# Routing from unnormed, weighted activations with the norm's factor applied per token, and a first gather in plain fp32

## What is computed

```python
for i in range(2):
    h = h + mixer_i(rmsnorm_2(h, norm_mix[i]))
    h = h + hier_moe(rmsnorm_2(h, norm_ffn[i]), ...)       # touched
    gate = sigmoid(rmsnorm_2(h, norm_ple[i]) @ w_ple_gate[i] + b_ple_gate[i])
    h = h + gate * (p[i] @ w_ple[i])

def rmsnorm_2(x, g):
    return x * rsqrt(mean(x * x, axis=-1) + EPS) * g

def hier_moe(x, w_rg, b_rg, w_re, b_re, w_gate, w_up, w_down):
    pg = softmax(x @ w_rg + b_rg)                # 4 groups, the best one is taken
    le = (x @ w_re + b_re) of that group         # 8 experts, the best two
    weight = pg_top * normalised(top_p)
    # each token's two experts: (silu(x @ w_gate[e]) * (x @ w_up[e])) @ w_down[e], weighted and summed
```

## Time and profile before

| | us |
|---|---|
| median of 3 runs | 1819.16 |
| lowest and highest | 1817.28, 1819.76 |
| the profiled execution, its own time | 1821.02 |
| its span in the trace | 1819.2 |
| PE busy | 1676.1 (92%) |
| DVE, ACT, POOL busy | 717.0, 512.0, 269.4 |
| mean granted TensorE clock | 0.965 |
| read from memory | 525.91 MB |

### The profile page before, as it was taken

One profiled execution on the slowest core, in us unless ns is written; L12 is line 12 of the kernel. 1 busy time (PEld: TensorE's weight loads), 2 busy tenths in 40 slices (PEclk: granted clock), 3 DMA queues, 4 the chain that ended last, 5 costly groups with the idle time before them and its releaser, 6 DMA issues.

```text
span 1819.2 us, 25704 instructions
## 1 busy us (share of the span) xinstructions
PE 1676.1 (92%) x10638; PEld 1141.4 (63%) x10638; DVE 717.0 (39%) x1356; ACT 512.0 (28%) x786; POOL 269.4 (15%) x165
## 2 busy tenths in 40 slices
PE   4989898999989999999999998897899999999986
PEld 2678597999989854454444545896655454443546
DVE  1466623899356531221212214667421221222224
ACT  3444334544343221111111114456211111111123
POOL 1405413477510010000000001000100000000010
PEclk9999979999999989999999999998999999999998
DMA  9203515343546759999999995333799999999960
GB/s 405 84 16 144 232 58 233 112 179 138 199 147 230 287 232 413 428 428 428 429 428 428 429 428 229 139 140 143 289 413 427 429 428 429 429 427 428 429 275 24
DMA packets 37516, 528.08 MB, mean 290 GB/s; under 512 B 4160, under 2 KB 4288, under 8 KB 4800
## 3 DMA queue, kind: packets, MB, share of 16 engines
q1 hardware_dynamic: 36864, 525.22, 69.9%
q10 hardware_dynamic: 576, 1.75, 0.2%
HBM read 525.91 MB, written 1.05 MB: 290 GB/s over the span
## 4 chain that ended last, share of the span: by engine, by line
PE 71%; DMA 16%; DVE 6%; ACT 5%; issue 1%; POOL 0%; SPq 0%; ACTq 0%; DVEq 0%
PE bank L500 24%; PE bank L988 18%; DMA ring<-in_w_up 13%; PE bank L1014 9%; PE bank L943 3%; PE bank L944 3%; PE bank L569 2%; PE bank L493 2%; PE bank L959 2%; DMA ring<-in_dense 2%; PE bank L960 1%; PE bank L1085 1%; DMA work<-in_dense 1%; PE bank L674 1%; ACT work L1443 1%
## 5 line engine op out<-in xcount | busy, mean ns | idle before, releaser
L988 PE MATMUL bank<-ring,work 128*64 128x512 f32 x1536 | 338.2, 595 | 14.6 <-DMA ring<-in_w_up 12.4
L500 PE MATMUL bank<-xn_rounded,ring_rounded 128*128 128x256 f32 (+1 forms) x2304 | 338.8, 290 | 9.4 <-DVE xn_rounded L1663 8.9
L500 PEld LDWEIGHTS bank<-xn_rounded,ring_rounded 128*128 128x128 f32 x2304 | 304.1, 196 | 14.7 <-issue 10.8
L988 PEld LDWEIGHTS bank<-ring,work 128*64 128x64 f32 x1536 | 112.6, 137 | 234.3 <-issue 220.6
L500 PE MATMUL bank<-work_rounded,ring_rounded 128*128 128x256 f32 (+1 forms) x1488 | 242.2, 297 | 12.4 <-DVE xn_rounded L1663 5.3
L1562 POOL TENSOR_TENSOR ring_rounded<-ring,ring_rounded 128x2048 fp32r<-128x2048 f32 (+1 forms) x43 | 187.0, 4369 | 292.9 <-ACT ring_rounded L1152 292.9
L500 PEld LDWEIGHTS bank<-work_rounded,ring_rounded 128*128 128x128 f32 x1488 | 208.1, 193 | 22.8 <-issue 7.9
L2140 DVE TENSOR_TENSOR work<-work,bank 128x512 f32<-128x512 f32 x32 | 22.0, 687 | 407.9 <-PE bank L988 407.9
L1014 PE MATMUL bank<-ring,work 128*64 128x512 f32 x768 | 170.1, 595 | 0.0
L1152 ACT ACTIVATE ring_rounded<-ring 128x2048 fp32r<-128x2048 f32 (+1 forms) x86 | 151.0, 1804 | 57.9 <-PE bank L500 36.0
L1632 POOL TENSOR_TENSOR work<-work_rounded,work 128x128 f32<-128x128 f32 x64 | 24.2, 399 | 838.4 <-PE bank L1007 831.4
(11 more groups left out here) (318 smaller groups left out, 1834.1 us busy)
## 6 DMA issues: line engine op xcount, KB each, us to landing
ring<-in_dense SPq DMA_DIRECT2D x50, 2048.0 KB, 8.6
ring<-in_w_gate SPq DMA_DIRECT2D x48, 2048.0 KB, 20.9
ring<-in_w_up SPq DMA_DIRECT2D x48, 2048.0 KB, 22.7
ring<-in_w_down SPq DMA_DIRECT2D x48, 2048.0 KB, 25.6
work<-in_w_gate SPq DMA_DIRECT2D x16, 2048.0 KB, 20.5
work<-in_w_up SPq DMA_DIRECT2D x16, 2048.0 KB, 24.1
work<-in_w_down SPq DMA_DIRECT2D x16, 2048.0 KB, 27.0
ring<-in_dense SPq DMA_DIRECT2D x8, 1408.0 KB, 6.2
```

Of the source, the lines that this page charges most:

```text
L500: last = mm(out, rv(ring[r][:, at:at + P]), rv(x[part][k]), start=k == 0 and j == 0, stop=k == n_k - 1 and j == 2)
L988: last = mm(b[64 * y:64 * y + 64, :], xg[:, k, 64 * y:64 * y + 64], ws[y][:, 512 * k:512 * k + 512], start=k == 0, stop=k == KT - 1)
```

## The change

- `add_output` (for `out_a` and `out_b`) now also makes the weighted, unnormed input hT * norm_ffn (two instructions behind each addition). `scaled` is no longer called ahead of the experts.
- The sums of squares become a column per 128 tokens: `token_sums` multiplies each 128 by 128 piece of squares with one column of ones. The reciprocal root is then 128 by 2 (`rstd_tok`).
- The first four tiles' sums and router products (`routing_ahead`) stand ahead of the last use of the projection.
- The logits are multiplied by `rstd_tok` per token where DVE adds the bias; the transposed tokens are multiplied by it in ACT's copy. That copy is fp32 alone. High and low parts are made behind the first gather (ACT and POOL), and wait for it.
- The first gather is 16 products in plain fp32. Two parts of the embedding stand ahead of it (one on each side of the rank products), two behind it.
- `select(0)` moves ahead of the overflow flag's five instructions and of six memsets; two casts, a copy and a subtraction go (a second table `iota1` in the constants, 32 KB more).
- `ple_w` gets a place of its own, and is loaded ahead of `odd`: in layer 0 once the first block's mixer has ended, in layer 1 once the first layer's experts have.
- Two semaphores of an earlier stage become one; its waits are the same.

```diff
-    ple_w, ple_sq, ple_xh = flat(2048, 2048), gsb, flat(0, 2048).rearrange("p (k t) -> p k t", k=KT)
+    ple_w, ple_sq, ple_xh = flat(17504, 2048), gsb, flat(0, 2048).rearrange("p (k t) -> p k t", k=KT)
...
-                sp.wait_ge(*((S["y_ready"], KT), (S["lru_var"], 3))[layer])
+                sp.wait_ge(*((S["h_ready"], KT), (S["moe_done"], 1))[layer])
                 sp.dma_start(ple_w, t["dense"][N_DENSE + layer][:, 0:2 * D]).then_inc(S["ple_w_load"], 16)
...
-            if layer:
-                load_embedding()
+            load_embedding()
             sp.wait_ge(*((S["h_ready"], 2 * KT), (S["lru_h"], KT))[layer])
             sp.dma_start(odd[0], gate[2]).then_inc(S["odd_full0"], 16)
             for c in order[len(early):]:
-                if layer == 0 and c == order[-2]:
-                    load_embedding()
                 load(base + c, (gate, up, down)[c // 2][c % 2], CHUNK)
...
-        projection("out_a", "w_out_a", 4, [[x[:, k] for k in range(KT)] for x in (yh, yT)], ("y_ready", 1), True)
+        w_r = par("w_router").rearrange("p (l k c) -> p l k c", l=2, k=KT)
+        def token_sums(tiles):
+            for k in tiles:
+                if k % 2 == 0:
+                    pe.wait_ge(S["sq_ready"], 4 * (count["norms"] + 1) + k // 2 + 1)
+                for u in range(NH):
+                    last = mm(bank[5][:, u:u + 1], sq1[:, k, P * u:P * u + P], ones[:, 0:1], start=k == u == 0,
+                              stop=k == KT - 1 and u == 1)
+            if tiles[-1] == KT - 1:
+                signal(last, "ss_ready")
+                count["norms"] += 1
+        def router(layer, tiles):
+            for k in tiles:
+                pe.wait_ge(S["xn_ready"], KT * n_normed[0] + k + 1)
+                last = mm(bank[7][0:36, 0:SEQ], w_r[:, layer, k], xs[k], start=k == 0, stop=k == KT - 1)
+            if tiles[-1] == KT - 1:
+                signal(last, "lg_mm")
+                n_normed[0] += 1
+        def routing_ahead(layer):
+            token_sums(early)
+            router(layer, early)
+        projection("out_a", "w_out_a", 4, [[x[:, k] for k in range(KT)] for x in (yh, yT)], ("y_ready", 1),
+                   lambda: routing_ahead(0))
...
-            ready = norm_input(late)
-            for b in range(BANKS):
-                released(pe, moe.last_use[layer] - b)
-
...
-            pe.wait_ge(S["p_load"], 16)
-            pe.wait_ge(S["ple_w_load"], 16 * (layer + 1))
-            embedded(2, 3)
-            w_r = par("w_router").rearrange("p (l k c) -> p l k c", l=2, k=KT)
-            for k in range(KT):
-                pe.wait_ge(S[ready[0]], ready[1] + k)
-                last = mm(bank[7][0:36, 0:SEQ], w_r[:, layer, k], xs[k], start=k == 0, stop=k == KT - 1)
-            signal(last, "lg_mm")
             def tokens(m):
+                released(pe, moe.last_use[layer] - 3 + m)
                 for i in range(4):
                     last = nc.tensor.transpose(bank[m][:, P * i:P * i + P],
                                                xnT[:, 4 * (m % 2) + i, P * (m // 2):P * (m // 2) + P], ident)
                 signal(last, "tok_mm")
+            router(layer, (4, 5))
             tokens(0)
+            token_sums(late)
+            router(layer, (6, 7))
+            tokens(1)
             pe.wait_ge(S["lg_sb"], layer + 1)
             for u in range(NH):
                 last = nc.tensor.transpose(bank[6][:, 36 * u:36 * u + 36], lgT[0:36, P * u:P * u + P], ident[0:36, 0:36])
             signal(last, "lg_cols")
-            tokens(1)
-            embedded(3, 4)
             tokens(2)
-            pe.wait_ge(S["ple_sb"], 4 * layer + 1)
             tokens(3)
-            embedded(0, 7)
+            pe.wait_ge(S["p_load"], 16)
+            pe.wait_ge(S["ple_w_load"], 16 * (layer + 1))
+            embedded(2, 4)
...
-            embedded(1, 6)
+            pe.wait_ge(S["tok_sb"], 4 * layer + 1)
+            embedded(3, 0)
...
-            pe.wait_ge(S["tok_low"], 4 * (layer + 1))
-            gather(0)
-            pe.wait_ge(S["ple_sb"], 4 * (layer + 1))
+            pe.wait_ge(S["tok_sb"], 4 * (layer + 1))
+            pe.wait_ge(S["onehot"], extra + 1)
+            for k in range(KT):
+                for u in range(NH):
+                    last = mm(bank[2 + k // 4][:, P * (k % 4):P * (k % 4) + P], xtok_low[:, u, k],
+                              rv(oneh[:, u].rearrange("p x s -> p (x s)")).bitcast(F32), start=u == 0, stop=u == NH - 1)
+            last.then_inc(S["gather_mm"], 1)
+            embedded(0, 7)
+            embedded(1, 6)
+            pe.wait_ge(S["ple_sb"], 4 * layer + 2)
...
+                pe.wait_ge(S["tok_low"], 2 * (layer + 1))
                 gather(i + 1)
...
-        sum_squares(early)
+        routing_ahead(1)
...
-            squares(hT, uses_free(USE[("out_a", "out_b")[layer]]))
+            squares(hT, uses_free(USE[("out_a", "out_b")[layer]]), sums=bank[5][:, 0:NH], rstd=rstd_tok)
...
-            embedded(2, 3)
             act.wait_ge(S["lg_mm"], layer + 1)
             signal(act.activation(lgT[0:36, :], bank[7][0:36, 0:SEQ], ACT.Copy), "lg_sb")
+            act.wait_ge(S["rstd_ready"], count["rstd_ready"])
...
-                act.activation(xtok_low[part], x, ACT.Copy)
-                signal(act.activation(rv(xtok_high[part]), x, ACT.Copy), "tok_sb")
+                signal(act.activation(xtok_low[part], x, ACT.Identity, scale=rstd_tok[:, m // 2:m // 2 + 1]), "tok_sb")
 
             tokens(0)
 
@@ -1424,18 +1450,22 @@
                 last = act.activation(rt(52, 4)[:, u], lg[:, u, 0:4], ACT.Exp, bias=rt(50, 1)[:, u], accum_out=rt(60, 1)[:, u])
             signal(last, "route_act")
             tokens(1)
-            embedded(3, 4)
+            tokens(2)
             act.wait_ge(S["route_dve"], 2 * layer + 2)
             signal(act.activation(rt(190, 1), rt(188, 1), ACT.Exp), "route_act")
-            tokens(2)
             tokens(3)
-            embedded(0, 7)
-            embedded(1, 6)
+            embedded(2, 4)
+            embedded(3, 0)
 
             done, extra = layer * PAIRS, layer * (PAIRS + 1)
             functions(SILU)
             act.wait_ge(S["gather_mm"], extra + 1)
             act.activation(xg[:, 0:4], bank[2][:], ACT.Copy).then_inc(S["xg_act"], 1)
+            embedded(0, 7)
+            embedded(1, 6)
+            for u in range(NH):
+                act.wait_ge(S["tok_sb"], 4 * layer + 2 * u + 2)
+                signal(act.activation(rv(xtok_high[:, u]), xtok_low[:, u], ACT.Copy), "tok_high")
...
-            for m in range(4):
-                pool.wait_ge(S["tok_sb"], 4 * layer + m + 1)
-                part = (slice(None), m // 2, slice(None), slice(64 * (m % 2), 64 * (m % 2) + 64))
-                x = xtok_low[part]
-                pool.tensor_tensor(rv(x), x, rv(xtok_high[part]), ALU.subtract).then_inc(S["tok_low"], 1)
+            pool.wait_ge(S["gather_mm"], extra + 1)
+            for u in range(NH):
+                pool.wait_ge(S["tok_high"], 2 * layer + u + 1)
+                x = xtok_low[:, u]
+                pool.tensor_tensor(rv(x), x, rv(xtok_high[:, u]), ALU.subtract).then_inc(S["tok_low"], 1)
...
+                released(dve, n)
+                for k in (2 * b, 2 * b + 1):
+                    signal(v.tensor_scalar(xnT[:, k], hT[:, k], par("norm_ffn", 8 * layer + k, 1), None, ALU.mult), "xn_ready")
...
-            scaled(hT, lambda k: par("norm_ffn", 8 * layer + k, 1), False)
...
+            for u in range(NH):
+                v.scalar_tensor_tensor(g8[:, u, 0:N_GROUPS], bank[6][:, 36 * u:36 * u + N_GROUPS], rstd_tok[:, u:u + 1],
+                                       bias[:, 0:N_GROUPS], ALU.mult, ALU.add)
+            for u in range(NH):
+                last = v.scalar_tensor_tensor(lg[:, u], bank[6][:, 36 * u:36 * u + 36], rstd_tok[:, u:u + 1], bias,
+                                              ALU.mult, ALU.add)
...
-            after(v.tensor_scalar(rankm[:, :, 0:E], rankm[:, :, 0:E], -1.0, None, ALU.add))
+            def select(pair):
+                for u in range(NH):
+                    last = v.tensor_tensor(rv(oneh[:, u]), iota1.unsqueeze(1).to_broadcast([P, 2, SLOTS]),
+                                           bc(rankm[:, u, bass.ds(pair * 2, 2)], [P, 2, SLOTS]), ALU.is_equal)
+                last.then_inc(S["onehot"], 1)
+            select(0)
...
-            select(0)
```

83 lines of the change are left out of this document (40 added, 43 removed).

## The result

The changed kernel took 1802.84 us (median of 4 runs, 1800.86 to 1805.69) against 1818.22 us for the kernel before on the same chip (4 runs, 1814.86 to 1819.76). The ratio is 0.9919, with a 95% interval from 0.9898 to 0.994: about 15 us faster, between 11 and 19. The forecast was 1810.8 us, 8.4 us faster, with a range down to 1804.5 us. The sign was right; the gain is nearly twice the forecast.

What follows compares the result with a forecast made beforehand. The expert loops were taken as bound by the weight stream, the stretch ahead of them mostly by TensorE. A 14.2 us gain at full clock minus 5.8 for clock falls gave 8.4: 1819.16 to 1810.8 us, range 1804.5 to 1816.

Steps and rivals of the forecast that it cites:

- The bound: Expert loops are paced by the weight stream; each us the first gate products end earlier is a us of the whole.
- E0 + 28.5: Predicted end of first gate products, in us after the old kernel's last output-projection product, at 2.4 GHz, in each layer.
- E + 9.0: Routing mask's time after the new end of the last output product; forecast 9.1 us, with a routing chain of 3.8 us.
- the wait: TensorE's wait for the routing mask, ahead of the rank products, was put at 1.4 us.
- the gather: First token gather: 16 fp32 products were to take 3.9 us, no change from 32 fp32r products at 3.8 us.
- the first gate product: Start of the experts' gate products, put 19.6 us after the new end of the last output product.
- The price of a one-column sum: Early and later token sums ahead of the routing: each priced at 0.23 us, from the 32-column rank product.
- at 2.4 GHz throughout: Gain from last output product to end of first gate products at full clock: 8.1 plus 6.1 us, 14.2 us in all.
- The clock takes some of it back: One fall of TensorE's clock expected per layer in the routing stretch, 2.9 us each, cutting the gain by 5.8 us.
- shorter waits: Layer 0's old clock fall was explained by 5.0 us of shorter waits and the rank products being enough.
- no fall of the clock: Rival: fp32 gather and missing waits keep the clock up in the routing, giving 1805.0 us; chance 0.15.
- a count of passes: Rival: first gather doubles by four fp32 passes, 3.8 us more per layer, giving 1818.4 us; chance 0.03.

Runs made afterwards that it cites:

- fill_wait: Changed kernel with one embedding part moved from behind the gather to ahead of the rank products, filling the mask wait; medians 1800.82 and 1802.15 us.
- late_select: Changed kernel with the first selection moved back behind the overflow flag's instructions and the six memsets; last output addition to first expert issue 30.41 us per layer.
- late_mask: Changed kernel with VectorE's six memsets moved from behind the first selection to ahead of the mask; 1819.09 us in one timed execution.
- pool_busy: Changed kernel with four added GpSimd subtractions during the routing, written where nobody reads; 1819.20 us in one timed execution.
- router_behind: Changed kernel with the first four router products back behind the last output product; last output addition to first expert issue 27.98 and 27.99 us.
- rounded_gather: Changed kernel with the first gather as 32 fp32r products again, low part left out; last output addition to first expert issue 26.25 and 26.26 us.
- before_fp32_gather: Kernel before with only the first gather as 16 fp32 products and GpSimd's low parts behind it; 1804.16 us, ratio 0.9933.

## Why the prediction was right and where it was wrong

**The bound, right.** What the first issue gained, the whole gained. Behind it the loops took what they had taken: from the first issue of layer 0 to the issue of `odd[0]` in layer 1 607.1 us before and 607.5 us after, and from the first issue of layer 1 to the end 506.0 and 504.7 us.

**The parts, right.** "E0 + 28.5" for the end of the first gate products came out at 41.30 - 12.99 = 28.3 us in layer 0 (12.99 us lay between the second and the last addition before) and at 38.16 - 9.66 = 28.5 us in layer 1 (9.66 us from the issue of `odd[0]` to the last addition), or 28.2 us by the first output addition. The mask stood at E + 9.0 (forecast 9.1), the wait was 1.3 us (1.4), the gather 3.73 us (3.9), the first gate product E + 19.1 (19.6). The price of a one-column sum, for which I had no row, was that of the 32-column product as chosen. The gain "at 2.4 GHz throughout", 14.2 us, is the 14.4 us of the traces.

**The step that failed** is the one under "The clock takes some of it back": "I take layer 1's 2.9 us for each". It measured 0 in both layers, in three traces. The reason given was that transposes, one-column sums and ranks are more short work than before. Short work alone did not bring the clock down (fill_wait: the same work without a wait, four layers, no fall). A fall came in every layer in whose routing TensorE had a wait of 1.9 us or more: six layers of six in late_select, late_mask and pool_busy, where the wait was added, and four of four in the two traces of the kernel before (1.9 us in layer 0, 3.3 us in layer 1). The changed order has none over 1.3 us. I had named the 3.3 us wait as what stood ahead of layer 1's fall, worked out that it would shrink to 1.4 us, and then kept its price. I had also read layer 0's fall from the sum of "shorter waits": it began at 646.0, half a microsecond behind the single 1.88 us wait for the one-hot matrix, which the change removes as well. The rival "no fall of the clock" was the result, and had a chance of 0.15.

**Two readings of rows were loose.** Layer 1's fall did not begin behind the 3.3 us wait but inside it, at 1294.4 to 1294.6 where the wait ends at 1295.43, and the clock was not back during the four fp32 embedding products but at 1301.4, 0.6 us into the gather behind them. And what GpSimd cost the routing chain was read in layer 0 and from the one cast of layer 1 that stood free; three others there were held up by 2.8 us. Neither enters the sum.

**The range** was too narrow at its lower end for a second reason. Even the case without a fall stood at 1805.0 us, and the median came out 2.2 us lower. The sum also started from a median of 1819.16 us for the kernel before, which with a fourth execution is 1818.22. Medians of the same kernel over 4 to 6 runs were 1802.84, 1804.76 and 1805.22 us here; the range had no term for that.

**The passes.** The fp32 gather took no longer than the fp32r one, 3.73 against 3.9 us. The Trainium skill (FP8 and Floating Point Precision, TensorE Precision Notes) gives true fp32 four passes through the array; a count of passes would have doubled the gather, and the trace does not bear that out for these products.

**What the change owes its gain to.** To the second half of its title far more than to the first. With the gather in fp32 and GpSimd's subtractions behind it alone, layer 1's way took 28.51 us instead of 34.62. The whole change with its router products behind the addition (router_behind) has 27.99, and from the first output addition it is 33.79 against 33.52 us with the whole change. So the norm per token, the early router products and the new place of the embedding's weights together brought 0.3 to 0.5 us there. Between the two parts of that small edit, rounded_gather and pool_busy decide, both tried in the changed kernel: the form of the gather changes nothing, GpSimd's subtractions in VectorE's way cost 5.7 us a layer. What the fp32 form gives is that the gather needs no low parts, so the subtractions can go behind it. In layer 0 the norm, router and embedding parts brought the remaining 3.3 us, through the earlier weights and the missing short fall; which of the parts did it was not tried apart. That the norm's eight instructions went from the way is true, but TensorE had had other work (embedding, router) beside them.

## What to carry to other kernels

Read a stretch as the busiest engine's work plus its waits plus what the clock adds, and ask of the clock which waits will be left, not what kind of work; 2.3 and 2.4 us of added wait cost 4.2 and 5.7 us here. The length of the wait does not give the length of the fall: the 1.9 us wait of the kernel before had the longest, 10.2 us. Look for small instructions that take five times their usual duration (0.93 against 0.17 us): another engine stands in their way, and moving that engine's work may be worth more than shortening the chain. If independent work is at hand, put it where the wait is: that was the last 3 us.

## What the runs showed of the hardware

- In both traces of the kernel before the falls of the clock stand some 21 and 16 us behind the last addition, although the stages ahead had shifted by 2 us. Falls came with waits of TensorE of 1.9 us (10.2 us long), 2.3 us (3.4 us long), 3.3 and 3.7 us (6.8 us long). One fall in twelve layers came behind a wait of 1.3 us, and one in before_fp32_gather at the end of another wait of 1.3 us; why those two came, and not the others, is left open.
- At half clock the fp32r gather of the kernel before ran some 6 us without the clock coming back, while in layer 1 it came back 0.6 us into the gather, behind four fp32 products with 256 columns. In late_select it came back within the fp32 gather, after 3.4 us.
- GpSimd held up VectorE's small instructions by up to 1.1 us each, whatever their size: with two inputs in memory (128x2 elements took 1.01 us instead of 0.16) and with one (a cast 0.93 us instead of 0.17, and L2092, a TENSOR_SCALAR, 1.26 us instead of 0.14 in layer 1).
- The stages ahead of the change moved by up to 9 us from run to run with the same code there (second output addition between 603.8 and 613.1 us over the eleven traces of the changed kernel and its variants), while the ways compared here repeated to 0.1 us in the changed kernel and 0.3 us in the one before.
